# Exponentials, normalising and the low weight half in another order, in a kernel of two attention layers, a mixer layer and a feed-forward layer

## The reference

```python
hn = _rmsnorm(x, ln)
proj = hn @ w_in                       # 2048 x 6656 (ab), 2048 x 8192 (c)
...
s = q @ k.T * dh ** -0.5 + bias        # 256 x 256 per head, 16 heads
p = softmax(s)                         # ab: the sink joins the sum for 8 heads
y = (p @ v) * silu(z)
x = x + y @ w_out                      # 2048 x 2048
```

## Time and profile before

| | |
|---|---|
| median of 3 runs | 2205.83 us (2204.28 to 2208.31) |
| the profiled execution's own time | 2204.19 us |
| its span, first to last instruction | 2202.3 us |
| TensorE busy (matmuls) | 2149.1 us, 98% |
| VectorE busy | 1363.2 us, 62% |
| ScalarE busy | 959.5 us, 44% |
| GpSimd busy | 214.8 us, 10% |
| mean granted TensorE clock | 0.991 |
| transfers, mean over the span | 175 GB/s |

### The profile page before, as it was taken

How to read it: one execution, slowest core, us unless ns; L and a number is a source line. 1 busy time by engine, 2 the same in 40 slices (tenths; PEclk the granted TensorE clock), 3 DMA queues, 4 the chain that set the end, 5 groups by cost and what they waited for, 6 DMA issues and landing times.

```text
span 2202.3 us, 29653 instructions
## 1 busy us (share of the span) xinstructions
PE 2149.1 (98%) x11831; PEld 1869.3 (85%) x11831; DVE 1363.2 (62%) x1454; ACT 959.5 (44%) x983; POOL 214.8 (10%) x242
## 2 busy tenths in 40 slices
PE   9999999999999999999999889999999999999997
PEld 8888888888888887888888878888888888888886
DVE  4666666455566666567788545666546765467654
ACT  5444445444343445454656224445433443334433
POOL 0101100003102200020000510002200022000200
PEclk9999999999999999999999899999999999999999
DMA  8755555656656556655545015655555565556553
GB/s 247 222 174 173 182 176 172 201 176 177 180 160 183 163 165 217 201 158 167 178 148 161 30 33 185 202 193 189 191 194 191 176 199 191 196 178 199 184 190 113
DMA packets 341136, 386.19 MB, mean 175 GB/s; under 512 B 26058, under 2 KB 287643, under 8 KB 340763
## 3 DMA queue, kind: packets, MB, share of 16 engines
q1 hardware_dynamic: 319979, 373.13, 52.7%
q10 hardware_dynamic: 21040, 11.35, 2.1%
HBM read 382.36 MB, written 4.00 MB: 175 GB/s over the span
## 4 chain that ended last, share of the span: by engine, by line
PE 88%; DVE 5%; ACT 3%; issue 1%; ACTq 1%; DMA 0%; SPq 0%; POOL 0%; DVEq 0%
PE acc L1414 38%; PE acc L1424 20%; PE acc L1449 7%; PE acc L1451 7%; PE acc L1450 7%; DVE w_lo L745 2%; ACT w_hi L374 2%; PE aux L1546 1%; ACTq L482 1%; PE aux L1701 1%; PE aux L1710 1%; PE acc L1488 1%; PE aux L1461 1%; PE acc L1709 1%; PE aux L1535 1%
## 5 line engine op out<-in xcount | busy, mean ns | idle before, releaser
L745 DVE TENSOR_TENSOR w_lo<-raw,w_hi 128x2048 fp32r<-128x2048 f32 x348 | 814.3, 2340 | 503.1 <-ACT w_hi L374 503.0
L374 ACT ACTIVATE w_hi<-raw 128x2048 fp32r<-128x2048 f32 x348 | 665.9, 1914 | 651.4 <-PE acc L1424 348.9
L1414 PE MATMUL acc<-act_x,w_hi 128*128 128x512 f32 x2496 | 609.1, 396 | 0.9 <-DVE act_x L854 0.9
L1414 PEld LDWEIGHTS acc<-act_x,w_hi 128*128 128x128 f32 x2496 | 463.8, 189 | 93.7 <-DVE act_x L854 1.3
L1414 PE MATMUL acc<-ff_x,w_hi 128*128 128x512 f32 x1536 | 366.6, 391 | 0.0
L1424 PEld LDWEIGHTS acc<-act_x,w_lo 128*128 128x128 f32 x2496 | 319.9, 191 | 12.0
L1414 PEld LDWEIGHTS acc<-ff_x,w_hi 128*128 128x128 f32 x1536 | 282.4, 188 | 54.7
L1424 PE MATMUL acc<-act_x,w_lo 128*128 128x256 f32 x2496 | 324.4, 283 | 0.0
L1424 PEld LDWEIGHTS acc<-ff_x,w_lo 128*128 128x128 f32 x1536 | 196.9, 191 | 7.5
L1449 PE MATMUL acc<-w_hi,act_x 128*128 128x512 f32 x512 | 200.0, 391 | 0.3 <-DVE w_lo L745 0.3
L1424 PE MATMUL acc<-ff_x,w_lo 128*128 128x256 f32 x1536 | 199.4, 283 | 0.0
(11 more groups left out here) (251 smaller groups left out, 1659.6 us busy)
## 6 DMA issues: line engine op xcount, KB each, us to landing
raw<-in_ffn_up SPq DMA_DIRECT2D x96, 1024.0 KB, 5.1
raw<-in_w_in_c SPq DMA_DIRECT2D x64, 1024.0 KB, 5.7
raw<-in_w_in_ab SPq DMA_DIRECT2D x52, 1024.0 KB, 5.0
raw<-in_ffn_down SPq DMA_DIRECT2D x48, 1024.0 KB, 5.0
raw<-in_w_in SPq DMA_DIRECT2D x40, 1024.0 KB, 5.2
raw<-in_w_out_ab SPq DMA_DIRECT2D x16, 1024.0 KB, 5.2
raw<-in_w_out_c SPq DMA_DIRECT2D x16, 1024.0 KB, 5.5
raw<-in_w_out SPq DMA_DIRECT2D x16, 1024.0 KB, 5.0
```

Source lines behind the costliest of these rows:

```text
L374: copy = lambda out, in_, **k: nc.scalar.activation(out, in_, ACT.Copy, **k)
L745: tt(w_lo[:, c % 2], raw[:, c], w_hi[:, c % 2].bitcast(F32), ALU.subtract).then_inc(lo_ready, 1)
L1414: mm(out(j), wide(w_hi[:, c % 2])[:, k, j * P:(j + 1) * P], x[:, 8 * r + k, :, :].rearrange("p a s -> p (a s)"), start=(r == 0 and k == 0) ...
```

## The change

Three orders are changed; no instruction is added or removed.

- `exps` issues `load_bias` after the exponentials and not before them.
- VectorE's `panel` gets a hook `before`, called at the start of each c. `attend` returns it beside `between`, and it calls `normalise` at c = 1 and 3, now ahead of the evacuation and of the split. The callers pass both by name.
- `deproject` waits for `hi_ready`, does all 16 matmuls with `w_hi` (x_hi and x_lo in turn, for each k and t), waits for `lo_ready`, and then does the 8 with `w_lo`.

```diff
             def exps(layer, n, b):
...
-                if not isinstance(n, int) or n + 2 < HEADS:
-
-                    load_bias(layer, n + 2, b)
                 for t in range(NT):
                     ins = nc.scalar.activation(E(b)[:, t, :], T(b)[:, t, :], ACT.Exp, bias=nm(b)[:, t:t + 1],
                                                accum_out=rs(b)[:, t:t + 1])
                 if layer == 0:
                     ins = nc.scalar.activation(es(b), nm(b), ACT.Exp, bias=sinks[:, bass.ds(n, 1)])
                 ins.then_inc(probs_exp, 1)
+                if not isinstance(n, int) or n + 2 < HEADS:
+
+                    load_bias(layer, n + 2, b)
...
-            def panel(gp, out, between=None, late=False):
+            def panel(gp, out, between=None, before=None, late=False):
...
                 for c in range(4):
+                    if before:
+                        before(c)
                     if c == (2 if late else 1):
                         dve.wait_ge(w_used, 4 * gp + 2)
                         out(0)
...
-                    else:
-                        normalise(layer, n + b, b)
-                return between
+
+                def before(c):
+                    if c % 2 == 1:
+                        normalise(layer, n + c // 2, c // 2)
+                return {"between": between, "before": before}
...
+                        x = lambda v, k, t: v[:, 4 * c + k, t * P:(t + 1) * P]
                         pe.wait_ge(hi_ready, 4 * gp + c + 1)
+                        for k in range(QK):
+                            for t in range(NT):
+                                mm(out(t), x(hi, k, t), w_hi[:, c % 2, k, :], start=(c == 0 and k == 0), stop=False)
+                                mm(out(t), x(lo, k, t), w_hi[:, c % 2, k, :], start=False, stop=False)
                         pe.wait_ge(lo_ready, 4 * gp + c + 1)
                         for k in range(QK):
                             for t in range(NT):
-                                x_hi = hi[:, 4 * c + k, t * P:(t + 1) * P]
-                                x_lo = lo[:, 4 * c + k, t * P:(t + 1) * P]
-                                mm(out(t), x_hi, w_hi[:, c % 2, k, :], start=(c == 0 and k == 0), stop=False)
-                                mm(out(t), x_hi, w_lo[:, c % 2, k, :], start=False, stop=False)
-                                ins = mm(out(t), x_lo, w_hi[:, c % 2, k, :], start=False,
+                                ins = mm(out(t), x(hi, k, t), w_lo[:, c % 2, k, :], start=False,
                                          stop=(c == 3 and k == QK - 1))
                         ins.then_inc(w_used, 1)
```

More of the change, by code:

```diff
@@ L1276, in _ @@
                 panel(AT_AB + p, lambda h: to_tile(AB_PANELS[p][1], h, p),
-                      attend(0, AB_FIRST_HEAD[p]) if p in AB_FIRST_HEAD else None)
+                      **(attend(0, AB_FIRST_HEAD[p]) if p in AB_FIRST_HEAD else {}))
             finish(0, AT_AB + N_AB - 1, N_AB - 1)
@@ L1286, in _ @@
                     panel(6 * r + (AT_C + 3 + i), lambda h: to_tile(step * r + tile, h, N_AB + 3 + 6 * r + i),
-                          None if head is None else attend(1, 8 * r + head))
+                          **({} if head is None else attend(1, 8 * r + head)))
             finish(1, AT_C + N_C - 1, N_AB + N_C - 1)
```

## The result

The changed kernel takes 2184.65 us (median of 4, 2184.11 to 2187.73) beside 2205.51 for the kernel before: ratio 0.9911, interval 0.9899 to 0.9922, so 20.9 us less where 19.8 were forecast, and 1.35 us under the forecast time of 2186.0. The profiled span is 2182.9 us, 19.4 less.

A forecast was written before the change was run, and what follows sets the result against it. TensorE, busy 98% of the span, was taken as the bound, so only its standstills count: 14.9 us from attention plus 4.9 from out-projections, 19.8 in sum, pace 0, giving 2186.0 us, range 2176 to 2198.

The forecast's parts named there:

- What bounds: TensorE, busy 98%; in the second attention layer a chain from bias issue to normalise ends last before the probability transposes.
- Bias transfers behind the exponentials: In attention, exponentials start 2.6 us earlier in the second layer, about 0.4 in the first; later transfers cost 0.
- Normalise ahead: In attention, normalise uses VectorE's idle wait, ending 5 us before TensorE asks; evacuation up to 1.0 us later, cost 0.
- What the attention gains: Probability transposes: 11 waits of 15.7 us vanish, worth 13.6, plus 1.3 from the clock: 14.9 us.
- the discount of 0.19 us a wait: Transposes' loads take 0.58 us without a wait, 0.42 behind one, so each wait costs its idle time less 0.19.
- Out-projections: Low weight half last in each chunk: gains of 1.9, 2.3 and 0.7 us in the out-projections, 4.9 us together.
- the late transfer: Second layer's out-projection: next panel's first chunk arrives late, ScalarE waited 8.50 us; about 2 us of TensorE idle time stays.
- Pace: Reordered out-projection matmuls: spacing unchanged, 0 us taken; bound 12 us either way; pace up 0.06, down 0.08.
- Waits that move: Attention waits shift to tile copies or the copy of transposed probabilities; half of 14.9 us stays, about 2193.5; chance 0.12.
- rival 1: The attention waits move rather than vanish, to tile copies or the transposed probabilities' copy: about 2193.5 us; chance 0.12.
- Clock by alternating banks: Out-projections: alternating accumulators drop TensorE's clock, 1.36 us a chunk hit, 131 us for all 96, about 2317; chance 0.04.
- No action: Attention: exponentials are held by something other than the issue, only out-projections gain, 2201 us; chance 0.04.

The follow-up runs named there:

- doubled issues: Each layer c bias transfer cut in two: on the kernel before 2234.0 us, ratio 1.0127; on the changed kernel 2208.5 us, ratio 1.0023.
- the order with the fewest changes: Changed kernel with token halves as outer loop of both out-projection passes, 4 accumulator bank changes a chunk and not 16: 2185.10 us, ratio 0.9911.
- the run with the constants later: Changed kernel with the mixer layer's constants (load_middle, 2.3 MB) issued behind the second panel of layer c's out-projection: 2183.74 us, ratio 0.9906.

## Why the prediction was right, point by point

**What bounds.** Right. The chain ran through issue, exponentials, copy, evacuation, split and normalise. Doubling its first link lengthened the waits at its end by 20.6 us, and the chain doesn't appear after the change.

**Bias transfers behind the exponentials.** Right in that they cost nothing by landing later; issued a further hook later and doubled they cost nothing still. Two things were left out. Issue and computing overlap on ScalarE, so the copy comes 1.0 us earlier and not at the same time. And the table load, which I had on the path of two heads, moves ahead of the wait.

**Normalise ahead.** Right: it lies in VectorE's idle time, and no pass waits for `w_lo`. The margin I gave, 5.6 us for the low pass, is not the smallest. In the changed kernel that pass has 3.2 us at the fourth head, and ScalarE's split for the high pass has 2.0 us there; the prediction doesn't name the latter. The change as made stays inside it; the run with normalise alone and that with doubled issues step over it.

**What the attention gains.** Sized at 14.9 us: 13.6 from waits and 1.3 from the clock. The two stretches of the table measure 1.95 + 13.42 = 15.4; without the discount of 0.19 us a wait they would be 17.0. The slow pass is gone.

**Out-projections.** Sized at 4.9, measured 1.75 + 2.41 + 0.53 = 4.7, with the late transfer holding TensorE for 2.09 us where "about 2" was forecast. That a transfer was the limit there is shown by the run that moved 2.3 MB out of its way. One thing was luck: the sum has no term for the clock here, and in the run with the out-projections alone the granted clock did fall behind the remaining wait, and that place gained 0.63 us and not 2.4.

**Pace.** The value taken (no change) was right, the bound of 12 us was based on a misreading. I compared starts of matmuls (0.2266 us) with the distance of weight loads in a panel's pass (0.2213). Loads run ahead inside a pass. By the starts of matmuls in the timeline after, a panel has the out-projections' pace:

```profile
546.46 3.82 PE L1418 MATMUL acc<-act_x,w_hi 128*128 128x512 f32 x16
...
550.11 2.08 PE L1428 MATMUL acc<-act_x,w_lo 128*128 128x256 f32 x16
```

3.65 us / 16 = 0.228. There was no difference to explain, and the range was wider below and above than it needed to be.

**Rivals.** Waits that move: not in the changed kernel, but in both runs that left the issue ahead of the exponentials or put more issues on ScalarE's queue, where the wait went to the high pass. That is rival 1 with another place than the ones I named. Clock by alternating banks: refuted. The changed kernel's out-projections hold 0.227 us a matmul, and the order with the fewest changes gains nothing. The granted clock fell in an out-projection in two runs, once in the old order (normalise alone) and once in the new, each time right behind a wait of over 2 us for a late transfer. What the Trainium skill describes ("TensorE: Matmul & The Clock Gate", section "A second HAM failure mode: psum-queue depth-cycling") has no counterpart in these runs. No action: refuted by the row of the exponentials.

## What to carry to other kernels

When one engine is busy 98% of the span, list its standstills and follow each back to the first link that stands there by program order alone; on an engine with its own queue, small work that nobody waits for (here issues of transfers) belongs behind the work that somebody waits for. Two edits that shorten the same chain don't add, and the one that takes the waiting step out of the chain is worth more than the one that shortens a link. Before calling a delay free, list every operand of the next pass and take the smallest margin, the copy for the high pass as well as the split for the low one. And compare traces stretch by stretch: two kernels here differ from the kernel before by 3 us, with a higher granted clock, in a stretch that their edits don't touch.

## What the runs showed of the hardware that I had not expected

- ScalarE's queue issues a transfer while an activation runs: 545.18 for the issue, 545.17 for the activation. Each of the four takes about 0.65 us, and only the part that outlasts the exponentials (1.54 us before the copy) holds ScalarE up.
- The activation table load doesn't wait for the operand of its activation. It ran at 517.13, 4 us before the exponentials at 521.35, once nothing that waits stood in front of it.
- Whether the clock falls behind a standstill of TensorE doesn't follow from its length in these traces. Behind 3.44 us in the kernel before, the granted clock was 0.72 over 6 us, and a pass took 4.87 us for 3.5. Behind 2.62 us at 879.34 it stayed at 1.00, while behind 2.59 us at the same place in the run with normalise alone it was 0.78 over 6 us. The mixer has a standstill of 1.6 us that nothing edited: it left the clock alone in the changed kernel (988.95), and not in the run with the constants later (986.14). Their windows, in this order:

```profile
988.00:994.00 6.00, 5.05 (x25) 4.34 (x26) 5.00 (x13) 1.55 (x1) 0.00 (x0) 1.00 0.69 200
```

```profile
986.00:992.00 6.00, 5.86 (x21) 4.83 (x22) 4.30 (x9) 0.75 (x1) 0.00 (x0) 0.72 0.72 232
```

- What a fall costs: the pass behind 3.44 us lost 1.4 us. With doubled issues in the changed kernel a pass was stretched to about 5 us behind waits of 2.27, 2.93 and 4.00 us, and not behind others of 1.4 to 2.1. Where the clock falls, such a wait costs up to two thirds more than its length.
